# Hybrid decoder step on one core: expert outputs are added to the outputs by accumulating indirect DMAs instead of stored, gathered and combined

## The chip, the cores and the metric

The kernel runs on one core of a Trainium2 chip, in one launch. The time is that of the device in microseconds; of three runs of the kernel before the median is 1448.83 us (1443.56 to 1450.93). The core's engines work on instruction streams of their own and meet by semaphores: TensorE (PE in the rows) multiplies matrices, VectorE (DVE) and ScalarE (ACT) work on vectors, GpSimd (POOL) here mostly issues indirect DMAs, SyncE (SP) issues the direct ones. All DMAs move on the core's 16 DMA engines.

## The reference, cut to what matters

One layer of a decoder in float32 on 1024 prompt tokens and 64 sample tokens, width 1024: window attention and a convolution module, cross attention, then a mixture of experts. The change is in the last part:

```python
def hier_moe(h, w_rg, b_rg, w_re, b_re, w_gate, w_up, w_down):
    t = h.reshape(-1, D_MODEL)                       # 1088 tokens
    ...
    gate = jax.nn.softmax(top_v, axis=-1) * pg_sel   # top 1 of 4 groups, then top 2 of its 8 experts
    comb = jnp.einsum('tk,tke->te', gate, jax.nn.one_hot(eidx, N_EXPERTS))
    a = jnp.einsum('td,edf->tef', t, w_gate)         # 32 experts, 1024 -> 256
    b = jnp.einsum('td,edf->tef', t, w_up)
    act = jax.nn.silu(a) * b * comb[:, :, None]
    return jnp.einsum('tef,efd->td', act, w_down)    # 256 -> 1024
...
x = x + cross_attend(...)
x = x + hier_moe(rmsnorm(x, norm_ffn_g), ...)        # y_p (prompt), y_s (samples)
```

Each token has two experts, so 2176 rows of expert work come out, each scaled by its gate and added to its token's row of x.

## The kernel before, in words

Tokens come in 9 tiles (tile 0 the 64 samples, the others 128 prompt tokens each). Up to about 1017 us TensorE works through the projections, attention, convolution and cross attention. In the cross attention's loop each tile's logits go through the router on VectorE: `route_hot` finds the two experts, `route_rows` each row's rank within its expert (TensorE counts with triangular matrices), and `route_add` sums a table of which token stands at which rank of which expert. After the last tile the table is copied to `idx_i` and `route_ready` is signalled. The normalised rows lie in DRAM (`z3_scratch`), the residual x2 in SBUF and, for tiles 0 to 4, in `x2_scratch`.

The expert stage works in blocks of 128 rows. Four experts share three blocks: each of the first three has 96 rows of one block, the fourth ("shared") has the last 32 rows of all three. That makes 24 blocks. Rows beyond these 96 are overflow: 4 further blocks are always computed after the 24, and loops of up to 18 passes follow on each engine for overflow blocks that this input does not need.

For block n: GpSimd gathers 128 rows of z3 by `idx_i` (`gather`), TensorE transposes them (`turn_rows`, semaphore `zt4_done`), VectorE scales them (`take_rows`), TensorE multiplies gate and up weights (`gate_up`, 1 MB each per expert), ScalarE and VectorE make the activation (`activate`), TensorE transposes it and multiplies the down weights (1 MB, `down`), and ScalarE and VectorE copy half the output each into `YB[n%2]`. TensorE's program is interleaved: gate/up of block n+1, transposes of the activation of n, transposes of the rows of n+2, down of n. SyncE loads weights into four slots as they come free. It also stores `YB` into `y_scratch0..2` (8 blocks per scratch; the last one takes the rest), and fills the overflow part of the last scratch with zeros early in the kernel (11264 KB, line 494).

The combine pass: for each scratch, GpSimd gathers for each tile and each of the token's two experts the rows by `rows_i` into one of 6 buffers (`gather_y`), and VectorE adds gate times row to the tile in SBUF (`combine`, 54 in all). A token whose expert row lies in another scratch has an index out of bounds, and its row does not move. The passes over the first two scratches lie beside the blocks; the third follows the last block and SyncE stores each tile to the output. Gates, ranks and indices of the passes are computed by VectorE beside blocks 0 to 5 (`route_gates`, `route_slots`, `route_over`, `route_eids`, `route_passes`).

Of the kernel before, what the change touches and what calls it, by code (L numbers as in the profile page):

```python
# [6 lines left out]
D = 1024  # L7
# [18 lines left out]
EVEN, ODD = (NB + 1) // 2, NB // 2  # L26
PASSES, PER_PASS = 3, 8
CRING = 6
PAD_TOK, PAD_ROW = 4096.0, 60000.0
# [55 lines left out]

def weight_plan():
    need = []
    for q in range(NE // 4):
        need += [("e", 4 * q + 3)] + [("e", 4 * q + r) for r in range(3)]
    need += [("o", k) for k in range(STATIC_OVER)]  # L90
    uses = {}
    for n in range(NR):
        uses[n] = [("e", 4 * (n // 3) + n % 3), ("e", 4 * (n // 3) + 3)]
    for k in range(STATIC_OVER):
        uses[NR + k] = [("o", k)]
# [23 lines left out]
def build(nc, i, o):  # L119
# [7 lines left out]
    with ctx:  # L127
# [21 lines left out]
        gates = sb("gates", 2 * NT)  # L149
        idxs = sb("idxs", 4, i32)  # L150
        rows_i = sb("rows_i", PASSES * 2 * NT, i32)
# [91 lines left out]
        RO, RP3, RM, RR, RQ, IDXA = tt(2, NE), tt(2, NE), tt(NE), tt(2, 128), tt(2, NE), tt(NE)  # L243
# [9 lines left out]
        R_T9, R_PG, R_E2, R_EG = rt(NT), rt(NT), rt(NT), rt(NT, NG)  # L253
        R_CNT, R_GT, ROV, RBASE = rt(1), rt(8), rt(128), rt(33)
        R_RANK, R_EXP, R_BASE, R_FL, R_ROW = (rt(2 * NT) for _ in range(5))
        RE2, RG8, RE3, R_EID = rt(2 * NT, NE), rt(2 * NT, 8), rt(OVER, NE), rt(OVER)
        R_Q, R_LAST, R_PT = (rt(2 * NT) for _ in range(3))
        R_GE, R_PM = rt(PASSES + 1, 2 * NT), rt(PASSES, 2 * NT)
        assert _r[0] <= 4096
        RRO, RQO = view(G, 9216, 2 * NT, 128), view(G, 11520, 2 * NT, OVER)  # L260

        gm = dwT[:, 0:PASSES * 2 * NT]
# [10 lines left out]
        XS = [view(G, a, D) for a in (0, 1024, 2048, 3072, 8192)] + [XR[s % 4] for s in range(5, NT)]  # L273
        CY = [view(W, a + 1024 * r, D) for a in (12288, 28672, 36864) for r in range(2)]

# [4 lines left out]
        x2_d = nc.dram_tensor("x2_scratch", [NTOK, D], f32).ap()  # L280
        z3_d = nc.dram_tensor("z3_scratch", [NTOK, D], f32).ap()
        y_d = [nc.dram_tensor(f"y_scratch{g}", [PER_PASS * 128 + (OVER * 128 if g == PASSES - 1 else 0), D], f32).ap() for g in range(PASSES)]
# [4 lines left out]
        def tok_rows(t, s):  # L287

            return t[SEQ:NTOK, :] if s == 0 else t[(s - 1) * 128:s * 128, :]

# [7 lines left out]
        def ring(name, n):  # L298
# [15 lines left out]
            cy_used xs_in y_done dve""".split()}  # L314
# [67 lines left out]
        wgu_in, zg_in, y_out = ring("wgu_in", 4), ring("zg_in", 2), ring("y_out", 2)  # L382
        wdn_in, WDN_AFTER = wmk_in, 16
        cy_in = ring("cy_in", CRING)

        def comb_at(n):

            g, j = n // PER_PASS - 1, 3 * (n % PER_PASS - 2)
            return [] if g < 0 or g >= PASSES - 1 or j < 0 else [2 * NT * g + j + c for c in range(3)]
# [55 lines left out]
        def _(sp):  # L445
# [111 lines left out]
            for it in range(NT + 2):  # L557
# [23 lines left out]
                if 0 <= s2 < NT:  # L581
                    sp.wait_ge(M["x2_ready"], AFTER["x2_ready"] + 2 * s2 + 2)
                    if s2 <= 4:
                        sp.dma_start(tok_rows(x2_d, s2), XR[s2 % 4][0:rows_of(s2), :]).then_inc(x2_out[s2 % 4], 16)
# [15 lines left out]
            def store_y(n):  # L600
                sp.wait_ge(M["yb_readyA"], n + 1)
                sp.wait_ge(M["yb_readyD"], n + 1)
                g = min(n // PER_PASS, PASSES - 1)
                sp.dma_start(y_d[g][(n - PER_PASS * g) * 128:(n - PER_PASS * g + 1) * 128, :], YB[n % 2]).then_inc(y_out[n % 2], 16)

            over_e = {}

            def expert_id(w):
# [1553 lines left out]
```

## Time and profile before

| | |
|---|---|
| median of 3 runs | 1448.83 us |
| the profiled execution | 1450.07 us, span of its records 1448.2 us |
| TensorE busy | 1271.6 us, 88% |
| VectorE, ScalarE, GpSimd busy | 53%, 21%, 8% |
| moved by DMA | 238.27 MB |
| by the queue of GpSimd's DMAs | 17.85 MB |
| expert stage | 1038 to 1407 us |

The busy time of a matmul row is partly modelled. The span begins with the first instruction; all times in rows count from there. DMA share is the mean busy share of the 16 DMA engines.

### The profile page before, as it was taken

The page shows a single profiled execution, that of the slowest core. Times are in us where ns is not written, and L with a number is a line of the kernel's source. Part 1 is how long each engine was busy: PE and PEld are TensorE (multiplying, and loading weights), DVE is VectorE, ACT ScalarE, POOL GpSimd, SP SyncE. Part 2 cuts the span into 40 slices and gives each one's busy share as a digit, 9 for nine tenths or more (in the row PEclk, how much of TensorE's full clock was granted, in tenths as well). Part 3 has the DMA queues.
Part 4 walks back from the last instruction along what each step waited for, and adds up shares of the span by engine and source line. Part 5 has one row for each costly group of instructions (what it writes and reads, how often), then busy time and mean ns, then how long its engine had stood idle before and what let it go on. Part 6 is the DMA issues. An engine that isn't in the chain of part 4 may idle for free.

```text
span 1448.2 us, 17786 instructions
## 1 busy us (share of the span) xinstructions
PE 1271.6 (88%) x6455; PEld 644.4 (44%) x6455; DVE 768.9 (53%) x2207; ACT 308.5 (21%) x866; POOL 122.2 (8%) x171
## 2 busy tenths in 40 slices
PE   7989999999999767788999999997599999898970
PEld 3434545555455433443555655565333333233430
DVE  1118799999999981322444444453344224334416
ACT  1133344544453421120111111111001010011100
POOL 0000000000000001000000000000100032132104
PEclk9998999999999977898999999998699999999995
DMA  8796001200000302352005110001499999999916
GB/s 322 261 330 211 0 23 42 104 30 30 16 15 15 142 17 105 130 217 102 21 30 218 44 44 15 15 32 70 141 352 369 363 414 418 414 411 418 391 67 224
DMA packets 68320, 238.27 MB, mean 165 GB/s; under 512 B 14112, under 2 KB 28358, under 8 KB 54387
## 3 DMA queue, kind: packets, MB, share of 16 engines
q1 hardware_dynamic: 56235, 217.20, 39.2%
q0 software_dynamic: 11424, 17.85, 3.6%
q10 hardware_dynamic: 576, 2.10, 0.4%
q8 instruction: 52, 0.85, 0.2%
q14 instruction: 33, 0.27, 0.1%
HBM read 216.27 MB, written 45.77 MB: 181 GB/s over the span
## 4 chain that ended last, share of the span: by engine, by line
PE 69%; DVE 11%; DMA 7%; SPq 5%; issue 4%; ACT 3%; POOL 0%; DVEq 0%; POOLq 0%; ACTq 0%
PE bank L775 21%; PE bank L1194 12%; PE bank L1147 9%; PE bank L1201 7%; PE bank L976 4%; DVE W L1645 4%; SPq L496 3%; DMA W<-in_w_exp_down 3%; PE bank L1125 2%; PE bank L1085 2%; PE bank L1181 2%; PE bank L818 1%; DMA W<-in_w_mv 1%; DVE G L1589 1%; PE bank L1161 1%
## 5 line engine op out<-in xcount | busy, mean ns | idle before, releaser
L775 PE MATMUL bank<-W,G 128*128 128x512 f32 (+3 forms) x864 | 355.1, 567 | 4.2 <-DVE G L1589 3.4
L1645 DVE SCALAR_TENSOR_TENSOR W<-W,dwT 128x128 f32<-128x128 f32 (+1 forms) x1080 | 280.1, 336 | 0.0
L775 PEld LDWEIGHTS bank<-W,G 128*128 128x128 f32 (+1 forms) x864 | 158.9, 187 | 176.9 <-issue 170.7
L1194 PE MATMUL bank<-W 128*32 128x512 f32 (+1 forms) x1600 | 206.0, 611 | 12.7 <-issue 10.9
L976 PE MATMUL bank<-W 128*128 128x512 f32 (+1 forms) x288 | 130.2, 611 | 11.4 <-ACT W L1439 6.7
L1194 PEld LDWEIGHTS bank<-W 128*32 128x32 f32 (+1 forms) x1600 | 64.5, 116 | 149.5 <-issue 147.1
L1147 PE MATMUL bank<-W 128*128 128x512 f32 (+1 forms) x288 | 128.2, 599 | 0.8 <-DVE W L1907 0.6
L1201 PE MATMUL bank<-W 128*32 128x512 f32 (+1 forms) x800 | 107.2, 617 | 4.5 <-DMA W<-in_w_exp_down 3.6
L2078 DVE TENSOR_TENSOR W<-bank,cvec 128x512 f32<-128x512 f32 x56 | 36.3, 687 | 124.4 <-PE bank L1181 117.9
L976 PEld LDWEIGHTS bank<-W 128*128 128x128 f32 (+1 forms) x288 | 54.0, 190 | 81.6 <-issue 81.3
L664 POOL TENSOR_SCALAR st<-st 128x1 f32<-128x1 f32 (+3 forms) x41 | 8.0, 196 | 954.6 <-DVE st L1718 475.9
L1147 PEld LDWEIGHTS bank<-W 128*128 128x128 f32 (+1 forms) x288 | 52.0, 185 | 64.5 <-issue 64.4
L2092 DVE SCALAR_TENSOR_TENSOR G<-W,dwT,G 128x1024 f32<-128x1024 f32 (+1 forms) x54 | 69.0, 1277 | 18.0 <-issue 13.5
L2112 DVE COPY W<-bank 128x512 f32<-128x512 f32 x28 | 19.4, 692 | 111.3 <-PE bank L1201 103.4
L1537 ACT ACTIVATE W<-bank 128x256 f32<-128x256 f32 x28 | 10.8, 384 | 241.4 <-PE bank L1223 241.4
L715 POOL DMA_INDIRECT W<-y_scratch,rows_i x54 | 54.7, 1013 | 79.2 <-DMA y_scratch<-W 59.3
L1201 PEld LDWEIGHTS bank<-W 128*32 128x32 f32 (+1 forms) x800 | 29.7, 116 | 61.7 <-issue 60.2
L706 POOL DMA_INDIRECT W<-z_scratch,idx_i x28 | 27.9, 998 | 265.4 <-PE bank L1181 245.7
L1373 ACT ACTIVATE W<-W,st 128x256 f32<-128x256 f32 (+2 forms) x68 | 32.5, 478 | 49.4 <-DVE st L1699 49.4
L1474 ACT ACTIVATE W<-G 128x1024 f32<-128x1024 f32 (+1 forms) x9 | 9.5, 1057 | 151.1 <-DVE G L1966 151.1
L1911 DVE TENSOR_REDUCE st<-bank 128x2 f32<-128x512 f32 x16 | 11.1, 692 | 53.4 <-PE bank L1085 53.4
L1125 PE MATMUL bank<-W,G 128*128 128x128 f32 x256 | 33.2, 292 | 4.2 <-DVE W L1922 4.2
(294 smaller groups left out, 1374.4 us busy)
## 6 DMA issues: line engine op xcount, KB each, us to landing
W<-in_w_exp_gate SPq DMA_DIRECT2D x36, 1024.0 KB
W<-in_w_exp_up SPq DMA_DIRECT2D x36, 1024.0 KB
W<-in_w_exp_down SPq DMA_DIRECT2D x36, 1024.0 KB
y_scratch<-W SPq DMA_DIRECT2D x28, 512.0 KB
y_scratch<-LG SPq DMA_DIRECT2D x1, 11264.0 KB
W<-in_cache_mem_k SPq DMA_DIRECT2D x8, 1024.0 KB, 5.5
W<-in_cache_mem_v SPq DMA_DIRECT2D x8, 1024.0 KB, 8.1
W<-in_w_in SPq DMA_DIRECT2D x4, 1792.0 KB, 25.9
```

The source lines that it names most:

```text
L496: sp.dma_start(o["swa_k_s"][0, :, 0:128 - DEC_T], i["cache_swa_k"][0, :, DEC_T:128]).then_inc(M["moved_out"], 16)
L715: pool.indirect_dma_start(out=CY[q % CRING][0:rows_of(s), :], out_offset=None, in_=y_d[g], in_offset=bass.IndirectOffsetOnAxis(ap=rows_i[0 ...
L775: mm = pe.matmul(bank[0:rows, at:at + hi - lo], HT[:, c, 0:rows], w[:, c, lo:hi], start=(c == 0), stop=(c == DC - 1))
L976: mm = pe.matmul(B[half][0:n3, :], lhs, w_out[:, c, 512 * half:512 * half + 512], start=(c == 0), stop=(c == 7))
L1125: mm = pe.matmul(B[6 + c // 4][:, (c % 4) * 128:(c % 4) * 128 + 128], MV[:, mt, c * 128:(c + 1) * 128], PT2[:, mt, c // 2, :], start=(mt = ...
L1147: mm = pe.matmul(B[2 + half][0:n2, :], OT2[:, c, 0:n2], w_mo[:, c, 512 * half:512 * half + 512], start=(c == 0), stop=(c == DC - 1))
L1194: mm = pe.matmul(B[2 + par][lo:hi, :], HG[par][:, c, lo:hi], WGU[u][:, :, c, :], start=(c == 0), stop=(c == DC - 1), skip_group_check=True)
L1201: mm = pe.matmul(B[6 + half][lo:hi, :], AT[par][:, c, lo:hi], WD[u][:, c, 512 * half:512 * half + 512], start=(c == 0), stop=(c == 1), ski ...
L1373: act.activation(sh, sh, ACT.Exp, bias=st[:, 50 + h:51 + h], scale=SCALE, accum_out=st[:, 58 + h:59 + h]).then_inc(M["s_exp"], 2 if s2 == ...
L1645: dve.scalar_tensor_tensor(y, src, w, y, ALU.mult, ALU.add).then_inc(M["conv_tap"], 1)
L2078: dve.tensor_tensor(buf[:, 4 * half:4 * half + 4, :], B[half][:, :].rearrange("p (c t) -> p c t", c=4), gain(V_FFN + 4 * half, 4), ALU.mul ...
L2092: dve.scalar_tensor_tensor(XS[s][0:n, :], CY[q % CRING][0:n, :], gm[0:n, at:at + 1], XS[s][0:n, :], ALU.mult, ALU.add).then_inc(M["cy_used ...
```

## The change

1. The rows of x2 of all nine tiles are stored directly to the outputs `y_p` and `y_s` (`y_rows`). Expert rows are then added there: `add_rows` issues two indirect DMAs with `compute_op=ALU.add` from `YB`, one into the 1024 rows of the prompt's output, one into the 64 rows of the samples'. Each skips the rows whose index is out of its bounds. `y_scratch`, `rows_i`, `gather_y`, `combine`, the reload of x2, the final stores and the zero fill are gone.
2. A token's two rows must not be added at once, so an expert block is added in two parts (rows 0 to 95 by `idx_i`/`samp_i`; then all 128 with an index table `part_i` that is out of bounds in the first 96), and each part waits until all adds before have landed (`yp_added`, `ys_added`). Overflow blocks go in one part. GpSimd adds block n-3 in its step n, behind the gather for block n+2.
3. ScalarE and VectorE wait for the adds of block n-2 before they write `YB[n%2]`, where they waited for its store.
4. The gate is multiplied into the activation (`activate`, `gate_s`). For this it is computed for each tile in the router (`gate_exp` on ScalarE, five steps in `route_rows`) and carried in the table beside the token; the steps after the last tile grow by the samples' index, the parts' indices and the gates.
5. The four overflow blocks stand after the fourth to the seventh group of three (`block_order`), with the weight loads in that order; SyncE frees the down weights' slot on `dn_done` instead of the output copies.

```diff
+def block_order():
+    order = []
+    for q in range(NE // 4):
+        order += [("e", 3 * q + r) for r in range(3)]
+        if 3 <= q < 3 + STATIC_OVER:
+            order.append(("o", q - 3))
+    return order
...
+        def parts_of(n):
+
+            return [(0, 128)] if BLOCKS[n][0] == "o" else [(0, WIDE), (WIDE, 128)]
+
+        def adds_through(n):
+
+            return sum(len(parts_of(m)) for m in range(n + 1))
...
-            sp.wait_ge(M["dve"], 1)
-            zeros = LG[:, None, 0:256].to_broadcast([128, OVER * 4, 256])
-            sp.dma_start(y_d[PASSES - 1][PER_PASS * 128:, :].rearrange("(p n) (q d) -> p (n q) d", p=128, d=256), zeros).then_inc(M["moved_out"], 16)
...
+            def add_rows(lo, hi, at_p, at_s, buf):
+
+                pool.indirect_dma_start(out=yp_flat, out_offset=bass.IndirectOffsetOnAxis(ap=at_p, axis=0), in_=buf[lo:hi, :], in_offset=None,
+                                        bounds_check=SEQ - 1, oob_is_err=False, compute_op=ALU.add).then_inc(M["yp_added"], 16)
+                pool.indirect_dma_start(out=ys_flat, out_offset=bass.IndirectOffsetOnAxis(ap=at_s, axis=0), in_=buf[lo:hi, :], in_offset=None,
+                                        bounds_check=NS - 1, oob_is_err=False, compute_op=ALU.add).then_inc(M["ys_added"], 16)
+
+            def add_block(n):
+
+                at, done = block_column(n), adds_through(n - 1) if n else 0
+                pool.wait_ge(M["yb_readyA"], n + 1)
+                pool.wait_ge(M["yb_readyD"], n + 1)
+                for lo, hi in parts_of(n):
+                    if done:
+                        pool.wait_ge(M["yp_added"], 16 * done)
+                        pool.wait_ge(M["ys_added"], 16 * done)
+                    if lo:
+                        add_rows(0, hi, part_i[:, at:at + 1], part_i[:, NR + at:NR + at + 1], YB[n % 2])
+                    else:
+                        add_rows(0, hi, idx_i[0:hi, at:at + 1], samp_i[0:hi, at:at + 1], YB[n % 2])
+                    done += 1
...
-            for n in range(NB - 2):
-                pool.wait_ge(M["zt4_done"], 2 * n + 2)
-                gather(idx_i[:, n + 2:n + 3], zg_in[n % 2], ZG[n % 2])
-                for q in comb_at(n):
...
+            for n in range(NB + 3):
+                if n + 2 < NB:
+                    pool.wait_ge(M["zt4_done"], 2 * n + 2)
+                    if BLOCKS[n + 2] == ("o", 0):
                         pool.wait_ge(M["over_ready"], 1)
+                    at = block_column(n + 2)
+                    gather(idx_i[:, at:at + 1], zg_in[n % 2], ZG[n % 2])
+                if n == 3:
+                    pool.wait_ge(M["gate_ready"], 1)
+                    for k in range(4):
+                        pool.wait_ge(x2_out[k], 16 * len(range(k, NT, 4)))
+                if n >= 3:
+                    add_block(n - 3)
...
+            def gate_exp(s4):
+
+                lg = LG[0:rows_of(s4), 36 * s4:36 * s4 + 36]
+                act.wait_ge(M["r_hot"], AFTER["r_hot"] + s4 + 1)
+                act.activation(T_EXP[0:rows_of(s4), :], lg[:, 0:NG], ACT.Exp, accum_out=T_GATE[0:rows_of(s4), 0:1])
+                act.activation(T_GATE[0:rows_of(s4), 1:2], lg[:, 4:5], ACT.Exp).then_inc(M["r_exp"], 1)
...
                 if n >= 2:
-                    act.wait_ge(y_out[p], (n // 2) * 16)
+                    act.wait_ge(M["yp_added"], 16 * adds_through(n - 2))
+                    act.wait_ge(M["ys_added"], 16 * adds_through(n - 2))
...
+            def activate(p, e, a, gate):
+
+                return dve.scalar_tensor_tensor(by_row(a, 2), B[2 + p][:, FE:2 * FE].rearrange("p (f c) -> p f c", c=2), gate,
+                                                e.rearrange("p (f c) -> p f c", c=2), ALU.mult, ALU.mult)
```

GpSimd's program in the middle of the expert stage, before: `zt4_done` is the transposes of an earlier block's rows, `cy_used` a combine on VectorE that frees a buffer.

```order
L706 DMA W<-z_scratch,idx_i 128x1024 [waits zt4_done] x11
L715 DMA W<-y_scratch,rows_i 64x1024 [waits y_out1,y_out0,over_ready]
L715 DMA W<-y_scratch,rows_i 64x1024
L715 DMA W<-y_scratch,rows_i 128x1024
L706 DMA W<-z_scratch,idx_i 128x1024 [waits zt4_done]
L715 DMA W<-y_scratch,rows_i 128x1024 x3
L706 DMA W<-z_scratch,idx_i 128x1024 [waits zt4_done]
L715 DMA W<-y_scratch,rows_i 128x1024 [waits cy_used] x3
```

And now, from the fourth block's gather on: `yp_added` and `ys_added` are the landings of the adds before.

```order
L701 DMA W<-z_scratch,idx_i 128x1024 [waits zt4_done] x4
L707 DMA out_y_p<-W,idx_i 1024x1024 [waits x2_out3,x2_out2,yb_readyA,x2_out1,yb_readyD,x2_out0,gate_ready]
L709 DMA out_y_s<-W,samp_i 64x1024
L707 DMA out_y_p<-W,part_i 1024x1024 [waits ys_added,yp_added]
L709 DMA out_y_s<-W,part_i 64x1024
L701 DMA W<-z_scratch,idx_i 128x1024 [waits zt4_done]
L707 DMA out_y_p<-W,idx_i 1024x1024 [waits yp_added,ys_added,yb_readyD,yb_readyA]
```

In place of one gather and, in some steps, three gathers of outputs, each step of GpSimd holds a gather and four adding DMAs, the third behind a wait for the first two and the next step's first behind a wait for the last two.

GpSimd's end of the program, before: the body's end and the closing of the loop over further overflow blocks (L739, L740; `idxs` is the index column of such a block), and what follows it.

```order
L706 DMA W<-z_scratch,idxs 128x1024 [waits idx_copied]
L746 ISA
L740 UNCONDITIONAL_BRANCH [waits y_out0]
L739 REGISTER_ALU
L739 COMPARE_AND_BRANCH
L715 DMA W<-y_scratch,rows_i 64x1024 [waits cy_used,y_out1,y_out0]
L715 DMA W<-y_scratch,rows_i 64x1024 [waits cy_used]
L715 DMA W<-y_scratch,rows_i 128x1024 [waits cy_used] x16
L127 UNCONDITIONAL_BRANCH
```

And now, the last block's adds, the reading of the number of blocks (L748) and the entry of the loop (L749, L750), behind whose close only the final branch is left.

```order
L707 DMA out_y_p<-W,part_i 1024x1024 [waits ys_added,yp_added]
L709 DMA out_y_s<-W,part_i 64x1024
L748 TENSOR_LOAD eid_i [waits zg_in0,zt4_done,ys_added,yp_added]
L748 ISA x2
L749 UNCONDITIONAL_BRANCH
L750 COMPARE_AND_BRANCH
L751 ISA
```

The 18 gathers behind the loop are gone; the loop itself, which stood ahead of the last stores' landing, now stands behind the landing of the last adds.

## Rows read from the trace of the kernel before

**Rows 1.** The page's busy line and its chain that ended last, by engine.

```profile
PE 1271.6 (88%) x6455; PEld 644.4 (44%) x6455; DVE 768.9 (53%) x2207; ACT 308.5 (21%) x866; POOL 122.2 (8%) x171
...
PE 69%; DVE 11%; DMA 7%; SPq 5%; issue 4%; ACT 3%; POOL 0%; DVEq 0%; POOLq 0%; ACTq 0%
```

**Rows 2.** Stretches: from:to, length, busy time by engine, PE clock, DMA share, GB/s.

```profile
1038.00:1407.00 369.00, 346.34 (x2708) 128.93 (x2708) 133.60 (x237) 35.29 (x84) 61.13 (x62) 0.96 0.89 355
1052.00:1352.00 300.00, 281.97 (x2454) 101.82 (x2446) 117.41 (x213) 28.90 (x69) 58.17 (x59) 0.97 0.99 395
1040.00:1060.00 20.00, 19.06 (x166) 6.42 (x162) 3.12 (x5) 1.20 (x3) 1.98 (x2) 0.94 0.53 190
1352.00:1400.00 48.00, 46.08 (x158) 21.14 (x154) 13.56 (x19) 5.07 (x13) 0.99 (x1) 1.00 0.53 217
1406.00:1448.20 42.20, 0.00 (x0) 0.00 (x0) 23.68 (x19) 0.00 (x0) 19.29 (x18) 0.56 0.62 207
```

**Rows 3.** Timeline of TensorE, one block: start, duration, line, [idle before <- releaser].

```profile
1061.04 7.05 PE L1194 MATMUL bank<-W 128*32 128x512 f32 x64
...
1068.29 1.04 PE L1181 MATMUL bank<-cst,W 128*128 128x128 f32 x8
...
1072.71 7.05 PE L1194 MATMUL bank<-W 128*32 128x512 f32 x64
```

**Rows 4.** Timeline of the tail: last output copy, first gather, first combine.

```profile
1405.90 0.69 DVE L2112 COPY W<-bank 128x512 f32<-128x512 f32 x1 [6.47 <-PE bank L1201]
1410.13 0.93 POOL L715 DMA_INDIRECT W<-y_scratch,rows_i  x1 [48.07 <-DMA y_scratch<-W]
...
1420.12 16.56 DVE L2092 SCALAR_TENSOR_TENSOR G<-W,dwT,G 64x1024 f32<-64x1024 f32 x12 [13.53 <-issue]
```

**Rows 5.** The zero fill: SyncE's next issue, ScalarE's wait, and two stretches.

```profile
77.62 41.53 SPq L496 DMA_DIRECT2D out_swa_k_s<-in_cache_swa_k  x1
...
132.93 1.06 ACT L1285 ACTIVATE W<-G 128x1024 f32<-128x1024 f32 x1 [16.39 <-DMA G<-in_x_prompt]
...
100.00:120.00 20.00, 15.57 (x112) 8.94 (x111) 12.95 (x53) 8.26 (x25) 0.00 (x0) 0.74 1.08 376
120.00:140.00 20.00, 19.10 (x56) 10.00 (x54) 19.13 (x95) 5.98 (x11) 0.00 (x0) 1.00 0.54 171
```

**Rows 6.** Timeline of GpSimd: one of several indirect DMAs in a row.

```profile
1340.26 0.99 POOL L715 DMA_INDIRECT W<-y_scratch,rows_i  x1 [0.30 <-issue]
```

**Rows 7.** Direct DMAs: KB each and median landing; the block stores by their line.

```profile
G<-x_scratch SPq DMA_DIRECT2D x12, 512.0 KB, 4.3
...
z_scratch<-W SPq DMA_DIRECT2D x8, 512.0 KB, 2.9
...
L604 SPq DMA_DIRECT2D y_scratch<-W x28: 326/327/349, 1062.1 to 1406.7; - x28
```

**Rows 8.** Landing of z gathers (L706): from 1000 to 1040, 1040 to 1060, all.

```profile
DMA to landing us min/median/max: 4.9/4.9/4.9
...
DMA to landing us min/median/max: 7.9/7.9/7.9
...
DMA to landing us min/median/max: 4.9/9.0/11.4
```

**Rows 9.** Timelines of VectorE, ScalarE and TensorE around the router's steps.

```profile
830.24 0.69 DVE L1927 COPY W<-bank 128x512 f32<-128x512 f32 x1 [2.12 <-PE bank L1125]
...
1024.95 0.19 DVE L1815 TENSOR_TENSOR W<-W 128x32 f32<-128x32 f32 x1
...
1026.37 0.22 DVE L1824 TENSOR_TENSOR W<-W,bank 128x64 f32<-128x64 f32 x1 [1.15 <-PE bank L1019]
...
1029.76 0.17 DVE L1850 CAST idx_i<-W 96x24 int32<-96x24 f32 x1
...
1029.29 0.23 ACT L1528 ACTIVATE G<-LG 128x36 f32<-128x36 f32 x1 [18.42 <-DVEq L2072]
...
1035.44 1.94 PE L1181 MATMUL bank<-cst,W 128*128 128x128 f32 x8 [4.08 <-DMA W<-z_scratch,idx_i]
```

More of the change, by code:

```diff
@@ L83, in rows_of, with block_column @@
     return NS if s == 0 else 128
-def weight_plan():
[L87 to L95, printed above, removed]
+def block_order():
[5 more added lines that the diff above has]
+    return order
+BLOCKS = block_order()
+def block_column(n):
+    kind, k = BLOCKS[n]
+    return k if kind == "e" else NR + k
+def weight_plan():
+    need, uses = [], {}
+    for n, (kind, k) in enumerate(BLOCKS):
+        if kind == "o":
+            uses[n] = [("o", k)]
+        else:
+            uses[n] = [("e", 4 * (k // 3) + k % 3), ("e", 4 * (k // 3) + 3)]
+        need += [w for w in reversed(uses[n]) if w not in need]
     last = {w: n for n, ws in uses.items() for w in ws}
@@ L620, in _ @@
             for n in range(NB):
-                if n == OVER_AT + 2:
-                    sp.wait_ge(M["over_ready"], 1)
-                    for s in range(5):
-                        sp.dma_start(XS[s][0:rows_of(s), :], tok_rows(x2_d, s)).then_inc(M["xs_in"], 16)
                 if n + 1 < NB and FREED[n + 1]:
@@ L1466, in _ @@
                     sum_sq(NT + 2, rows_of(0), XR[0])
[L1469 to L1471 removed]
+            def gate_exp(s4):
[3 more added lines that the diff above has]
+                act.activation(T_GATE[0:rows_of(s4), 1:2], lg[:, 4:5], ACT.Exp).then_inc(M["r_exp"], 1)
+            for it in range(NT + 3):
+                s1, s2, s3, s4 = it, it - 1, it - 2, it - 3
+                if 0 <= s4:
+                    gate_exp(s4)
+                if 0 <= s3 < NT:
                     n3 = rows_of(s3)
@@ L1814, in route_hot @@
                     link(dve.tensor_tensor(RO[0:n, k, :].rearrange("p (g e) -> p g e", g=NG), bc(og, EPG, 2), bc(T_O[0:n, k, :], NG, 1), ALU.mult))
+                link(dve.tensor_tensor(lg[:, 4:5], top[:, 2:3], top[:, 1:2], ALU.subtract))
                 dve.tensor_tensor(RM[0:n, :], RO[0:n, 0, :], RO[0:n, 1, :], ALU.add).then_inc(M["r_hot"], 1)
-                dve.tensor_tensor(lg[:, 4:5], top[:, 2:3], top[:, 1:2], ALU.subtract).then_inc(M["dve"], 1)
-                steps[0] += 1
             def route_rows(s4):
                 n = rows_of(s4)
-                keep = LG[0:n, 36 * s4 + 5:36 * s4 + 9]
+                keep, gate = LG[0:n, 36 * s4 + 5:36 * s4 + 9], LG[0:n, 36 * s4 + 9:36 * s4 + 11]
+                part = T_GATE[0:n, :]
+                dve.wait_ge(M["r_exp"], AFTER["r_exp"] + s4 + 1)
+                link(dve.tensor_scalar(part[:, 2:3], part[:, 1:2], 1.0, part[:, 0:1], ALU.add, ALU.mult))
+                link(dve.reciprocal(gate[:, 0:1], part[:, 2:3]))
+                link(dve.tensor_tensor(gate[:, 1:2], gate[:, 0:1], part[:, 1:2], ALU.mult))
+                for k in range(2):
+                    link(dve.tensor_scalar(RQ[0:n, k, 1, :], RO[0:n, k, :], gate[:, k:k + 1], None, ALU.mult))
+                link(dve.tensor_scalar(RQ[0:n, :, 0, :], RO[0:n], tok[0:n, s4:s4 + 1], None, ALU.mult))
                 dve.wait_ge(M["r_rank"], AFTER["r_rank"] + s4 + 1)
```

237 lines of the change are left out of this document (84 added, 153 removed).

## The prediction, as it was recorded before the changed kernel ran

> **What bounds the kernel now.** I read the page's busy shares and chain first, then the stretches, the timeline of one block, the landings of the indirect gathers, and last the two places where the removed passes show. TensorE is busy 88% and holds 69% of the chain [rows 1]. The expert stage runs from 1038 to 1407 us: TensorE is busy 346.3 of 369 us, so it idles 22.7 there, with the DMA engines at a share of 0.89, and of 0.99 from 1052 to 1352 [rows 2]. A block of expert rows costs TensorE 11.7 us (gate/up starts at 1061.04, the next at 1072.71) [rows 3]. After the last block comes a tail without TensorE, 42.2 us [rows 2]: the last copy at 1405.90 (0.69 us), 13.53 us in which VectorE only runs through its loop over overflow blocks that don't occur, then the last combine pass [rows 4].
>
> **What is removed.** (a) The tail's combine: from 1420.1 to 1448.2, 28 us. (b) 54 gathers and 54 combines, 28 stores of 512 KB (14.7 MB), and the zero fill of 11.5 MB. In the stage the combines lie beside TensorE; what they cost is within the 22.7 us of idle time. (c) The zero fill blocks SyncE for 41.53 us, and ScalarE waits 16.39 us for a prompt tile behind it, but TensorE is busy 15.57 and 19.10 us of the 20 in the two stretches around it [rows 5]; its idle there is mostly after VectorE rows. I count 1 us gained (bounds 0 and 5.3, all the idle time of the two stretches).
>
> **What is added.** Each block's output is now added from SBUF into the two output tensors by GpSimd. The 24 expert blocks come in two parts (rows 0 to 95, then the shared expert's 32), the 4 overflow blocks in one: 52 parts, each of two DMAs, one into the prompt's output and one into the samples', most of whose rows are out of bounds. Before each part GpSimd waits until both adds of the part before have landed. Queued behind that wait are the other part, the gather for a later block, and with it everything: ScalarE and VectorE may only write block n's output when the adds of block n-2 have landed, VectorE's next activation stands behind that copy, and TensorE's transposes behind the activation.
>
> So a chain of its own arises on GpSimd. Let t be the time from the issue of a part's first add to the landing of its second. A block takes 2t plus one gather's issue, 0.99 + 0.30 = 1.3 us [rows 6]; TensorE takes 11.7. The chain decides if t is over 5.2 us. **What t is** no row of before shows, so it is bounded:
> - from below: two issues are 1.3 us apart [rows 6], and a plain store releases its waiter 3.4 us after its issue on idle DMA engines (1406.7 to 1410.13) [rows 4, 7]. 4.7 us.
> - from above: 1.3 us plus the slowest gather, 11.4 us [rows 8]. 12.7 us. A read-modify-write that takes a gather and then a store one after the other would be 1.3 + 9.0 + 3.4 = 13.7.
> - near rows: the same kind of indirect DMA, a gather of 128 rows, lands 4.9 us after issue when the engines are nearly idle, 7.9 us in the stretch from 1040 to 1060, where the DMA share is 0.53, 9.0 in the median [rows 2, 8]. So already the pair of weight loads that belongs to a block makes it slow.
>
> With t = 8 an expert block takes 17.3 us. Three of them use four experts, 12.6 MB, so 243 GB/s of weights, and adds and gathers on top: which makes about 290: a share of some 0.7 where 395 GB/s go with 0.99 [rows 2], between the rows of 7.9 and 9.0 us. Against that: a part moves at most 96 or 32 rows where a gather has 128, and a plain store lands in 2.9 us where a plain load of that size takes 4.3 [rows 7]. For more: the second add's 1.3 us, the gather queued ahead, the tiny packets of out-of-bounds rows, and the reading of the destination. I take t = 8, by the 7.9 row.
>
> The Trainium skill ("DMA: Bandwidth & Descriptors", section "Anatomy of one DMA") gives a GpSimd DMA about 2.0 us plus bytes over 436 GB/s; for 96 rows of 4 KB that would be an estimated 2.9 us, t near 4 and no GpSimd chain at all, which is the first rival. The trace disagrees as far as it goes: the gather's 4.9 and 9.0 us [rows 8] stand against its 3.2 for 128 rows. The same page, section "Queues, rings and completion order", lets each DMA engine go round its queues packet by packet; by that, light packets still wait their turns behind weight packets, and t stays near 8 although few bytes move.
>
> **The router's additions.** Gates are now computed for each tile: 2 exponentials on ScalarE (one of 0.23 us stands in the rows) and 5 small VectorE steps of about 0.2 us. For eight tiles they fit in VectorE's 2.12 us of idle time before its copy at 830.24. For the last they stand on the path: the mask leaves at 1025.1, VectorE goes on at 1026.37; exponentials and five steps would end about 1 us later. Then come 16 small copies of 0.17 us, 2.8 us, and route_bases, some ten steps; TensorE waits for the first gather until 1035.44 anyway [rows 9]. Cost 1 us (bounds 0 and 3.8). Of route_slots and route_passes many steps go; what TensorE waited for them goes too, but under a GpSimd chain it is worth nothing, for what is late next is the adds. The same holds for the overflow blocks placed between the groups: it evens the weight loads (their share is 0.53 after 1352 against 0.99 before [rows 2]), a gain only if TensorE or weights decide.
>
> **The sum**, on the profiled execution: the transposes of block 3 end at 1069.3 [rows 3]; router +1, a gather's issue +1.3: the first add goes out at 1071.6. Then 52 t, and 23 gathers x 1.3 = 29.9. Behind the last landing GpSimd still runs its loop over absent overflow blocks; I take VectorE's 13.5 us for it [rows 4], bounds 5 and 20. Zero fill -1, outside the span +1.9 (1450.07 less 1448.2; that execution is 1.2 over the median of the runs). Together 1115.9 + 52 t: for t = 8, 1532 us. It meets 1450 at t = 6.43, so the cost of the change is almost wholly 52 times what t exceeds 6.4.
>
> **Rivals.**
> 1. Adds are cheap, t of 5.2 or less, TensorE stays the bound. For: the 4.9 us gather, the 2.9 us stores, 14.7 MB less stored. Against: all landings of 7.9 and more beside weights. Time: last copy at 1406.6, less most of the 22.7 us idle (17), router +1: 1390.6; then two parts of 5 and the loop, 1414; with -1 and +1.9, 1415 us. Between t = 5.2 and 6.3 the chain decides and the time, up to 1443 us, is still below before. Faster.
> 2. A read-modify-write costs both trips, t = 13.7: 1828 us; from t = 11 on (1688) I count this case. For: the destination is read first, and nothing in the trace shows an accumulating DMA. Against: reading and writing of many rows overlap in each gather too.
> 3. The blocks' lag of three and the chain balance, t 6.3 to 6.55: no change, within 0.5% of the time (7 us, about what a measurement of this kernel can tell). That the adds fail to replace the passes is no rival: the diff leaves no combine.
>
> **Chances.** My forecast, t from 6.55 to 11, 1457 to 1688: 0.64, likeliest about 1530; its own range is 1475 to 1640. Rival 2, 0.11. Rival 3, 0.04. Faster by over 0.5% (rival 1 with its band), 0.21: that this band is not smaller comes from the two rows for idle engines, since a slower stage also loads them less. Slower by over 0.5% is 0.64 + 0.11 = 0.75. The range 1412 to 1680 leaves out about 1 in 10 above and the lower half of rival 1 below.
>
> **What would show it.** Right: GpSimd's adds follow at about 8 us a pair, ScalarE's and VectorE's waits before the output copies fall on the adds' DMAs, TensorE's rows come every 17 us with waits before the transposes of the activation, the DMA share in the stage is about 0.7, weights are never waited for, and after the last add there is a stretch of some 13 us without work. Wrong: TensorE at 11.7 us a block with adds landing within 5 us (rival 1), or a DMA share below 0.5 and pairs 13 us apart (rival 2). If t is as forecast but the total is not, the GpSimd loop or the 1 us terms are off.

## The result, and the profile after

The changed kernel takes 1564.54 us in the median of 4 runs (1559.12 to 1569.9), the kernel before 1447.98 (4 runs beside them): a ratio of 1.0813, 95% interval 1.079 to 1.0835. The forecast was 1532 with a range of 1412 to 1680, and slower by over 0.5% at 0.75. The profiled execution took 1569.9 us, its span is 1567.8. The executions of one kernel given here lie within 1% of one another, so where a time below comes from one run, a difference of 56 us or more is far outside that.

The page's busy line, then its chain of work by engine and by line:

```profile
PE 1293.0 (82%) x6455; PEld 654.9 (42%) x6455; DVE 717.2 (46%) x2206; ACT 311.5 (20%) x891; POOL 226.3 (14%) x221
...
DMA 0%
DMA out_y_s<-W,part_i 0%
```

GpSimd (POOL) works 226 us where it worked 122, and VectorE 52 us less [rows 1]: the combines are gone. The page's chain, which before gave TensorE 69%, now names one single add and stops there, so it says nothing of the stage. (It does so in the runs without the empty loop too; why is not known.) A chain that breaks off like this is a reason to go to the waits. These are the waits from 1030 us on (engine, tile and line that waited; releaser; us in total, times, longest):

```profile
ACT W L1560 <- DMA out_y_s<-W,part_i: 309.6, 21, 22.2
DVE W L2103 <- DMA out_y_s<-W,part_i: 277.3, 21, 20.9
...
POOL out_y_p L707 <- DMA out_y_s<-W,samp_i: 133.7, 22, 11.3
POOL out_y_p L707 <- DVE W L2103: 120.3, 23, 9.4
PE bank L1236 <- DVE W L2086: 111.1, 21, 12.9
```

Read from below upwards this is the chain that was forecast: TensorE's transposes of the activation wait for VectorE's activation, that stands behind VectorE's output copy (L2103), and this waits for the adds of two blocks back, as ScalarE's copy (L1560) does. GpSimd waits between the parts of a block for an add. Between blocks the profile names VectorE's copy, but that is the copy of a later block, for which GpSimd doesn't wait: the landing that released the copy is the one that GpSimd waited for (below). No wait for weights is in the whole list.

The chain itself on GpSimd, in the first two blocks and at the end (start, duration, line, [idle before it <- releaser]):

```profile
1071.55 0.99 POOL L701 DMA_INDIRECT W<-z_scratch,idx_i  x1 [10.69 <-PE bank L1194]
1072.84 1.49 POOL L707 DMA_INDIRECT out_y_p<-W,idx_i  x1 [0.30 <-issue]
1074.63 1.43 POOL L709 DMA_INDIRECT out_y_s<-W,samp_i  x1 [0.30 <-issue]
1087.35 1.56 POOL L707 DMA_INDIRECT out_y_p<-W,part_i  x1 [11.29 <-DMA out_y_s<-W,samp_i]
1089.21 1.56 POOL L709 DMA_INDIRECT out_y_s<-W,part_i  x1 [0.30 <-issue]
1091.08 1.06 POOL L701 DMA_INDIRECT W<-z_scratch,idx_i  x1 [0.30 <-issue]
1098.89 1.46 POOL L707 DMA_INDIRECT out_y_p<-W,idx_i  x1 [6.75 <-DVE W L2103]
...
1534.81 1.56 POOL L707 DMA_INDIRECT out_y_p<-W,part_i  x1 [4.59 <-DMA out_y_s<-W,samp_i]
1536.68 1.56 POOL L709 DMA_INDIRECT out_y_s<-W,part_i  x1 [0.30 <-issue]
1540.78 1.42 POOL L707 DMA_INDIRECT out_y_p<-W,idx_i  x1 [2.54 <-DMA out_y_s<-W,part_i]
1542.51 1.42 POOL L709 DMA_INDIRECT out_y_s<-W,samp_i  x1 [0.30 <-issue]
1547.35 1.56 POOL L707 DMA_INDIRECT out_y_p<-W,part_i  x1 [3.42 <-DMA out_y_s<-W,samp_i]
1549.22 1.56 POOL L709 DMA_INDIRECT out_y_s<-W,part_i  x1 [0.30 <-issue]
```

The landings of the adds into the samples' output (L709), those of the adds into the prompt's (L707), and ScalarE's copy that waited for the same landing as GpSimd's issue at 1098.89:

```profile
DMA to landing us min/median/max: 2.7/6.1/11.9
...
DMA to landing us min/median/max: 2.7/6.2/11.7
...
1098.08 0.60 ACT L1560 ACTIVATE W<-bank 128x512 f32<-128x512 f32 x1 [16.07 <-DMA out_y_s<-W,part_i]
```

Four things stand in these rows. An adding DMA occupies GpSimd for 1.42 to 1.56 us, the gather for 0.99 to 1.06. From the first add of a part to the first add of the next it takes 14.5, 11.5 us beside weights, 6.0 and 6.6 us at the end, where the weights are all in. A landing is not yet the next issue: the add of 1089.21 lands 8.8 us later, at 1098.0, ScalarE starts at 1098.08, and GpSimd's next add at 1098.89, 0.9 us after the landing; over all parts this step takes 0.84 us at least and 0.89 in the mean. And nothing follows 1549.22 until the span's end at 1567.8. Counted to where a next issue would begin, the last part ends at about 1553.3, if it takes the 4.1 us of the row 1536.68 to 1540.78; so 52 parts take 1553.3 - 1072.84 = 480.5 us, 9.24 us each, and 14.5 us without work follow.

The stage until 1500 (from:to, length, busy time of TensorE, weight loads, VectorE, ScalarE, GpSimd, then TensorE's granted clock, DMA share, GB/s):

```profile
1038.00:1500.00 462.00, 353.09 (x2607) 136.94 (x2609) 89.62 (x186) 32.14 (x77) 161.45 (x115) 0.87 0.73 252
```

TensorE now idles 109 of 462 us and its granted clock is 0.87 instead of 0.96 [rows 2]. The lower clock goes with the gaps: from 1085 to 1093 us it is 1.00, while TensorE waits until 1104.7 it is 0.50, and in the 7.3 us of work behind that 0.70. TensorE's rows behind a gap take longer for it (below), but TensorE waits after them all the same, so the clock is not what sets the time.

TensorE, one block (start, duration, line, [idle before it <- releaser]):

```profile
1085.84 7.05 PE L1207 MATMUL bank<-W 128*32 128x512 f32 x64
1104.79 0.69 PE L1236 MATMUL bank<-cst,W 128*128 128x128 f32 x2 [11.90 <-DVE W L2086]
1105.28 1.91 PE L1194 MATMUL bank<-cst,W 128*128 128x128 f32 x8
1107.12 4.57 PE L1214 MATMUL bank<-W 128*32 128x512 f32 x32
```

Against [rows 3], gate/up (64 matmuls) still take 7.05 us, but behind them TensorE waits 11.9 us; after that wait the eight transposes take 1.91 us instead of 1.04 and the down product 4.57 where 3.64 is common. The wait is a long one because in this block VectorE also runs some 5.3 us of routing steps between its copy (1098.09) and the activation; in the mean of the waits listed above it is 5.3 us. From the first block's add (1072.84) to the last's (1540.78) it is 467.9 us for 27 blocks: 17.3 us a block.

### The profile page after: what moved, and what is told of

The parts are those of the page before. It is cut to its first block and busy times, and to the rows that moved or that the text cites. A ratio compares the mean times of both kernels' runs of the same rounds, so it can differ in the third digit from the quotient of the medians.

```text
span 1567.8 us, 17872 instructions
## 1 busy us (share of the span) xinstructions
PE 1293.0 (82%) x6455; PEld 654.9 (42%) x6455; DVE 717.2 (46%) x2206; ACT 311.5 (20%) x891; POOL 226.3 (14%) x221
## 3 DMA queue, kind: packets, MB, share of 16 engines
q0 software_dynamic: 17472, 17.92, 5.6%
## 5 line engine op out<-in xcount | busy, mean ns | idle before, releaser
L1207 PE MATMUL bank<-W 128*32 128x512 f32 (+1 forms) x1600 | 200.2, 599 | 1.7 <-DVE W L2082 1.7
L2103 DVE COPY W<-bank 128x512 f32<-128x512 f32 x28 | 19.3, 691 | 318.5 <-DMA out_y_s<-W,part_i 277.3
L1214 PE MATMUL bank<-W 128*32 128x512 f32 (+1 forms) x800 | 116.7, 665 | 0.9 <-ACT W L1554 0.9
L1236 PE MATMUL bank<-cst,W 128*128 128x128 f32 x56 | 15.4, 367 | 111.1 <-DVE W L2086 111.1
L1560 ACT ACTIVATE W<-bank 128x512 f32<-128x512 f32 x28 | 16.7, 597 | 352.8 <-DMA out_y_s<-W,part_i 309.6
L1236 PEld LDWEIGHTS bank<-cst,W 128*128 128x128 f32 x56 | 7.0, 170 | 135.3 <-DVE W L2086 131.7
L707 POOL DMA_INDIRECT out_y_p<-W,idx_i x28 | 41.7, 1489 | 129.0 <-DVE W L2103 120.3
L707 POOL DMA_INDIRECT out_y_p<-W,part_i x24 | 37.6, 1565 | 145.5 <-DMA out_y_s<-W,samp_i 133.7
L1194 PE MATMUL bank<-cst,W 128*128 128x128 f32 x224 | 41.1, 345 | 1.0 <-DMA W<-z_scratch,idx_i 1.0
L709 POOL DMA_INDIRECT out_y_s<-W,samp_i x28 | 40.4, 1444 | 8.5 <-issue 8.5
## 6 DMA issues: line engine op xcount, KB each, us to landing
W<-in_w_mv SPq DMA_DIRECT2D x4, 1024.0 KB, 13.5
```

What stands on the lines that cost most here:

```text
L707: pool.indirect_dma_start(out=yp_flat, out_offset=bass.IndirectOffsetOnAxis(ap=at_p, axis=0), in_=buf[lo:hi, :], in_offset=None, bounds_ch ...
L709: pool.indirect_dma_start(out=ys_flat, out_offset=bass.IndirectOffsetOnAxis(ap=at_s, axis=0), in_=buf[lo:hi, :], in_offset=None, bounds_ch ...
L1194: mm = pe.transpose(B[half][:, c * 128:(c + 1) * 128], ZG[u][:, k * 128:(k + 1) * 128], ident)
L1207: mm = pe.matmul(B[2 + par][lo:hi, :], HG[par][:, c, lo:hi], WGU[u][:, :, c, :], start=(c == 0), stop=(c == DC - 1), skip_group_check=True)
L1214: mm = pe.matmul(B[6 + half][lo:hi, :], AT[par][:, c, lo:hi], WD[u][:, c, 512 * half:512 * half + 512], start=(c == 0), stop=(c == 1), ski ...
L1236: mm = pe.transpose(B[4 + p][:, c * 128:(c + 1) * 128], AB[p][:, c * 128:(c + 1) * 128], ident)
```

## The experiments

**One part for each block.** The 52 parts exist because a block's rows 0 to 95 and its last 32 (the shared expert) can hold the same token, and the change keeps a token's two rows out of one DMA. Here the last 32 rows come from the group of experts two further on, whose tokens are others, so one part will do: 28 parts, the same rows and bytes. The filling of the second parts' index columns goes too.

```diff
-            uses[n] = [("e", 4 * (k // 3) + k % 3), ("e", 4 * (k // 3) + 3)]
+            uses[n] = [("e", 4 * (k // 3) + k % 3), ("e", 4 * ((k // 3 + 2) % 8) + 3)]
...
-            return [(0, 128)] if BLOCKS[n][0] == "o" else [(0, WIDE), (WIDE, 128)]
+            return [(0, 128)]
...
-                    a = dve.tensor_copy(slots[WIDE:128, :, r], table[PART * r:PART * r + PART, :, 3])
+                    dve.tensor_copy(slots[WIDE:128, 0:6, r], table[PART * r:PART * r + PART, 2:8, 3])
+                    a = dve.tensor_copy(slots[WIDE:128, 6:8, r], table[PART * r:PART * r + PART, 0:2, 3])
```

> The changed kernel, but the shared expert of each group of three blocks is taken from the other expert group two places on, so that no token stands twice in a block and every block is added in one part: 28 parts in a chain instead of 52, the same rows. If the chain of parts on GpSimd decides (9.2 us a part now), a block needs one part and a gather's issue, 9 to 11 us, which is less than TensorE's 11.7: TensorE decides again, last output copy near 1395, then a part and the loop, 1405 to 1445 us. Rival: the adds cost by rows and bytes (read-modify-write), not by their number; 2176 rows stay, and the time stays at 1540 to 1570.

Measured: 1434.7 us (1431.41 to 1435.84, 4 runs), ratio to the kernel before 0.990, interval 0.9861 to 0.9939, a gain of 1%; 130 us less than the changed kernel, in the expected range. Its adds into the prompt's output, and its stretch of the stage:

```profile
L707 POOL DMA_INDIRECT out_y_p<-W,idx_i x28: 1552/1579/2158, 1074.1 to 1413.6; - x28
...
DMA to landing us min/median/max: 4.7/10.0/12.2
...
1038.00:1400.00 362.00, 341.93 (x2681) 125.70 (x2679) 90.59 (x189) 34.27 (x82) 107.93 (x77) 0.96 0.88 324
```

A block now takes (1413.6 - 1074.1) / 27 = 12.6 us, against TensorE's 11.7 [rows 3] and the 9 to 11 expected: the chain is still slightly longer than TensorE's work, and ScalarE's and VectorE's copies still wait for adds. The add even lands later (10.0 us in the median; 6.2 in the changed kernel). It has 128 rows where it had 96 or 32, and the DMA share is 0.88 where it was 0.73; which of the two makes it later was not tried apart. But there is one landing a block and not two. The count of landings in a row decides, for the rows that move and their bytes are the same. (The rows out of bounds, of which the second parts had many, fall too; the run with four targets below keeps them all and gains as much.)

**Only the prompt's adds.** Of the pair of DMAs of each part the one into the samples' output is left out, so that output lacks its experts' rows; the waits for it go with it.

```diff
-                pool.indirect_dma_start(out=ys_flat, ... compute_op=ALU.add).then_inc(M["ys_added"], 16)
```

> The changed kernel without the adds into the samples' output (the expert rows of the 64 sample tokens are left out); still 52 parts in a chain, each of one DMA. If a part costs two issues of 1.45 to 1.56 us and the landing of the second, each part falls by one issue and its gap, 1.8 us, and perhaps some of the landing: 52 x 1.8 to 2.5 us, so 1435 to 1470 us. Rival: the landing of the first, larger add decides and the second hides behind it; then less than 20 us go.

Measured: 1508.87 us in one run, 56 less than the changed kernel, 1.07 us a part. A miss for the expectation (1435 to 1470) and for its rival (less than 20 us): the step from one DMA to two was put too high. The adds that are left land in 7.3 us in the median where those into the prompt's output took 6.2 with the second behind them. The stage runs faster, its DMA share from 1038 to 1400 us rises from 0.75 to 0.81, and part of the saving is given back. In this run the page's chain doesn't break off: it gives TensorE 53% and DMAs 26%, where it gave 69% and 7% before [rows 1].

**Plain writes in place of adds.** The same DMAs without accumulation; where two blocks write a row, the last one stands and the sums are missing.

```diff
-                                        bounds_check=SEQ - 1, oob_is_err=False, compute_op=ALU.add).then_inc(M["yp_added"], 16)
+                                        bounds_check=SEQ - 1, oob_is_err=False).then_inc(M["yp_added"], 16)
```

> The changed kernel with the same indirect DMAs as plain writes (rows overwrite the outputs instead of being added), the same waits. If accumulating costs only the longer issue (1.45 to 1.56 against 1.0 us for a gather), parts fall by some 1 us and the time to 1505 to 1530. Rival: reading the destination first makes the landing; then each landing falls by 2 us or more and the time to below 1470. Second rival: nothing changes (1555 to 1570), the wait is that of any scatter.

Measured: 1505.48 us in one run, 59 less, the lower edge of the expected range. Its rows by line, and its end:

```profile
L707 POOL DMA_INDIRECT out_y_p<-W,idx_i x28: 917/928/1472, 1074.2 to 1481.4; - x28
L707 POOL DMA_INDIRECT out_y_p<-W,part_i x24: 982/988/1000, 1088.4 to 1486.1; - x24
...
DMA to landing us min/median/max: 2.1/6.0/11.4
...
1481.41 0.92 POOL L707 DMA_INDIRECT out_y_p<-W,idx_i  x1 [2.02 <-DMA out_y_s<-W,part_i]
...
1486.07 0.98 POOL L707 DMA_INDIRECT out_y_p<-W,part_i  x1 [2.52 <-DMA out_y_s<-W,samp_i]
1487.36 0.98 POOL L709 DMA_INDIRECT out_y_s<-W,part_i  x1 [0.30 <-issue]
```

Issues take 0.92 to 0.98 us, some 0.5 less than the adding ones. Beside weights the landing, counted from the issue's start, has nearly the same median (6.0 against 6.2); its mean is 5.9 against 6.9, and half of this 1.0 us is the longer issue itself. On idle DMA engines a part takes 4.7 us here (1481.41 to 1486.07) and 6.6 with adds (1540.78 to 1547.35): 1.0 of these 1.9 us are the two issues, 0.9 is left for the accumulation. With a last landing 3.0 us after 1487.36 (as from 1478.41 to 1481.41, one part earlier), the 52 parts take (1490.4 - 1074.2) / 52 = 8.0 us each, against 9.24. So accumulation, its longer issues included, is some 60 us of the time, and the chain of landings the larger rest: plain writes in the same chain are still 4% slower than the kernel before.

**Four targets.** The parts add in turn into four scratch tables, and a part waits for the part four back, so that no two DMAs in flight write the same table; the tables are not brought together at the end, so the expert rows are missing from the outputs.

```diff
-                    if done:
-                        pool.wait_ge(M["yp_added"], 16 * done)
-                        pool.wait_ge(M["ys_added"], 16 * done)
+                    if done >= 4:
+                        wait_part(pool, done - 4)
```

> The changed kernel with its 52 parts of two adds, but part j goes into scratch j mod 4 (the outputs keep x2 alone, the four sums are not brought together), so that GpSimd waits for the part four back instead of the last one; number, size, kind and queue of the DMAs stay. If the wait for the last landing makes the time, GpSimd needs 4 x 1.8 + 1.4 = 8.6 us a block, TensorE's 11.7 decide again, and the time is 1410 to 1440 us. Rival: the DMA engines can't do these adds faster beside the weights; then the time stays above 1520.

Measured: 1439.3 us in one run. GpSimd in the middle of the stage:

```profile
1197.80 1.46 POOL L718 DMA_INDIRECT tp_scratch<-W,idx_i  x1 [0.31 <-issue]
1199.56 1.43 POOL L720 DMA_INDIRECT ts_scratch<-W,samp_i  x1 [0.30 <-issue]
1201.29 1.57 POOL L718 DMA_INDIRECT tp_scratch<-W,part_i  x1 [0.30 <-issue]
1203.16 1.56 POOL L720 DMA_INDIRECT ts_scratch<-W,part_i  x1 [0.30 <-issue]
1210.27 1.06 POOL L712 DMA_INDIRECT W<-z_scratch,idx_i  x1 [5.54 <-PE bank L1204]
```

All 104 accumulating DMAs are still there, with the same issue times, and those into the prompt's tables land in 12.8 us in the median of the 39 whose landing the trace tells; but four go out back to back, and GpSimd then waits for TensorE (PE) and not for a landing. The page's chain gives TensorE 67% again. That is worth 125 us. It is the wait for each landing before the next issue that costs the time. (The four tables also change where rows are added; this can't be told apart from the shorter waits here.)

**No weights in the stage.** The weight loads of blocks after the first ones are left out (the matmuls run on stale weights).

```diff
-                for w in FREED[n]:
-                    load_down(sp, expert_id(w), WSLOT[w])
```

> The changed kernel without the weight loads of the expert stage: each block works on what lies in its slot (wrong experts for most), all else as before. If the landing is long because light packets share the DMA engines with the weights, a part falls from 9.2 us to the 6.5 us seen where nothing else moves, 52 x 2.7 = 140 us less: 1420 to 1455 us. Rival: a landing of 6 us belongs to the add itself; then the time stays above 1530.

Measured: 1437.8 us in one run, 127 less than the changed kernel. GpSimd, the landings of the prompt's adds, and the stretch:

```profile
1207.06 1.46 POOL L701 DMA_INDIRECT out_y_p<-W,idx_i  x1 [1.21 <-DVE W L2097]
...
1213.38 1.56 POOL L701 DMA_INDIRECT out_y_p<-W,part_i  x1 [3.13 <-DMA out_y_s<-W,samp_i]
...
1220.17 1.46 POOL L701 DMA_INDIRECT out_y_p<-W,idx_i  x1 [2.00 <-DVE W L2097]
...
DMA to landing us min/median/max: 2.7/5.0/6.6
...
1038.00:1400.00 362.00, 339.52 (x2710) 124.53 (x2708) 91.89 (x191) 35.30 (x84) 175.60 (x124) 0.96 0.27 47
```

These parts take 6.3 and 6.8 us from issue to next issue (1207.06, 1213.38, 1220.17); all take 6.7 in the mean and 8.5 at most, and the slowest landing is 6.6 us, against 11.7. A block takes 12.4 us, near TensorE's 11.7, and the time is 0.6% below that of the kernel before beside it (1446.49). The rest, 9.24 - 6.7 or 2.5 us a part, is the neighbourhood of the weights. It also speaks against the first rival: from a part's first issue to its second landing it takes 5.7 us in the mean, so that the rival's 5.2 isn't reached even on nearly idle engines, at a DMA share of 0.27.

**Overflow blocks last.** The four overflow blocks come behind the 24 others and not between the groups.

```diff
-        if 3 <= q < 3 + STATIC_OVER:
-            order.append(("o", q - 3))
+    order += [("o", k) for k in range(STATIC_OVER)]
```

> The changed kernel with the four overflow blocks after the 24 others again (only their order is undone). The number of parts is the same, so if the chain decides, the time stays within 8 us of 1564. Rival: spread weights shorten the landings, or the overflow blocks' order costs; then it moves by more than 10 us.

Measured: 1565.12 us (1558.79 to 1569.38, 4 runs), ratio to before 1.0808, interval 1.0774 to 1.0841; the changed kernel's is 1.0813. No difference, as expected: weight loads are not what is waited for, so their order is worth nothing here.

**The empty loop skipped.** On every engine the loop over further overflow blocks stands in a condition.

```diff
+            with pool.If(total > 1):
-            with pool.Fori(1, OVER - STATIC_OVER + 1) as n:
+                with pool.Fori(1, OVER - STATIC_OVER + 1) as n:
```

> The changed kernel with the loops over further overflow blocks inside one condition on each engine, so that they are passed over when there is none. If the 14 us after the last add are GpSimd's loop of 18 empty passes, the time falls by 12 to 14 us, to 1550. Rival: they are the landing of the last adds and the end of the program, and at most 2 us go.

Measured: 1554.25 us (1549.94 to 1557.56, 4 runs), ratio to before 1.0723 (1.068 to 1.0767), 10.3 us less than the changed kernel. In the trace the last add's issue is at 1547.07 and the span ends at 1555.5: 8.4 us later, in place of 18.6. Landing (4.1) and some 4 us of ending are left. So the loop is worth 10 us and not the 12 to 14 expected, and of the 14.5 us behind the last part 4 belong to what follows the loop.

**Both together.** One part for each block, and the loop skipped.

> One part per block (as in the run before of that name, 1434.7 us) and the loops over further overflow blocks behind one condition. The two act at different places (the chain of adds; the stretch behind the last add), so the condition gives again what it gave alone, 10 us: 1422 to 1428 us, faster than the kernel before by 1.5 to 2%. Rival: with the chain shorter another engine's loop or the end of the program holds the end, and less than 4 us come.

Measured: 1427.97 us (1425.74 to 1432.26, 6 runs), ratio to before 0.9876, interval 0.9854 to 0.9897: 1.2% less than the kernel before, at the upper edge of the expected range. The guard adds 3.5 to 7 us to the run with one part (by the ratios, by the medians), less than the 10 us that it gave alone. Its last issue on GpSimd, and the stage until 1400:

```profile
1415.89 1.55 POOL L710 DMA_INDIRECT out_y_s<-W,samp_i  x1 [0.30 <-issue]
...
1038.00:1400.00 362.00, 337.90 (x2642) 126.23 (x2642) 89.67 (x187) 33.02 (x79) 106.94 (x77) 0.96 0.89 324
```

TensorE is busy 338 of 362 us. The stage is no shorter than before: VectorE's last output copy begins at 1410.56, where it began at 1405.90 [rows 4]. What is saved is the tail: the last add goes out at 1415.89 and the span ends at 1426.0, where before the last combine pass and its stores held until 1448.2 [rows 2, 4].

**The same guard on the kernel before.** The loops skipped in the kernel before, nothing else, to see whose gain that is.

> The kernel before, with its loops over further overflow blocks skipped when there are none (the guard of e7 and e9), nothing else. It tells how much of e9's gain over the kernel before belongs to the adding DMAs and how much to the skipped loop. Theory A, from before's tail: VectorE's first combine starts at 1420.12 after 13.53 us in the loop, GpSimd's seventh gather of the last pass waits for the buffer that this combine frees (4.68 us), and the first six gathers need until 1417.5; without the loop the combine can start at about 1414, when the first gathers have landed, so GpSimd goes on without a gap and the end comes 4 to 6 us earlier: 1442 us (1440 to 1445). e9 then stays some 14 us faster than this. Rival: the loop is on the path with its whole 13.5 us, 1435 us, and more than half of e9's gain would be the guard. Second rival: nothing, since the gathers and the last stores set the end, 1448.

Measured: 1449.23 us (1446.1 to 1453.59, 12 runs), ratio 0.9993, interval 0.998 to 1.0007: nothing, the second rival of this expectation and not the 4 to 6 us of its main theory. Its tail:

```profile
1412.68 2.66 DVE L2096 SCALAR_TENSOR_TENSOR G<-W,dwT,G 64x1024 f32<-64x1024 f32 x2 [7.11 <-DMA W<-y_scratch,rows_i]
1412.97 1.87 POOL L716 DMA_INDIRECT W<-y_scratch,rows_i  x1 [0.30 <-issue]
...
1419.94 1.95 POOL L716 DMA_INDIRECT W<-y_scratch,rows_i  x1 [0.30 <-issue]
...
1436.13 1.08 POOL L716 DMA_INDIRECT W<-y_scratch,rows_i  x1 [0.30 <-issue]
```

VectorE's first combine starts at 1412.68 instead of 1420.12, as that theory had it (about 1414), and GpSimd no longer waits for a buffer. But its issues, which before took 0.93 to 1.14 us apart from the one behind the wait (1.46), now take up to 1.95 in the part where VectorE's combines run between them, and the last gather goes out at 1436.13, where it was 1437.85. The 13.53 us of [rows 4] were off the path: GpSimd's 18 gathers are the path there. So the guard gives the kernel before nothing, and the version with one part gains 1% without it (0.990); with the adds the loop stands on the path, and only there does the guard count. Why the issues stretched was not tried apart, nor was the other choice of shared experts on the kernel before.

## Why the prediction was right, and by how much it was off

**The mechanism** was as forecast, in each step: the adds form a chain on GpSimd of 52 parts; ScalarE's and VectorE's waits stand before the output copies; TensorE's rows come every 17.3 us (17 forecast) with waits before the transposes; the DMA share is 0.73 (0.7); weights are not waited for; the end is a stretch without work of 14.5 us (13.5). Three experiments cut the chain in different ways and each gives back 125 to 130 us: fewer landings, landings not waited for one by one, quicker landings.

**The sum** was 38 us short of the profiled 1569.9. By its terms: first add out at 1072.84, where router and zero fill together gave 1070.6 (+2.2); 52 parts with their gathers 480.5 us, where 52 x 8 + 29.9 = 445.9 were put (+34.6); the stretch behind them +1.0; outside the span +0.2.

- **t as it was defined** runs from a part's first issue to the landing of its second add. It was put at 8 and is 8.35 us in the mean of the 52 parts (4.6 to 13.7), +18 us together. This agreement is in part luck. The 8 was the landing of one gather, 7.9 us, and the second issue's offset stood only under "for more". Measured, that offset is 1.8 us (1072.84 to 1074.63) and not 1.3, because an accumulating issue is 0.5 us longer, and the second add lands 6.5 us after it in the mean.
- **From landing to the next issue** GpSimd needs 0.9 us, 46 us for 52 parts, and the sum had nothing for it. Of the forecast's numbers only the plain store's 3.4 us, used in its bounds, held this step, as they ran from the store's issue to its waiter's start; a gather's landing ends before it. So a link of the chain costs 8.35 + 0.89 = 9.24 us.
- **The 23 gathers at 1.3 us** were a double count. The gather's issue stands behind the second part's issue (1091.08 to 1092.14 in the rows above) and runs while that part lands; it lengthens a block only if the landing is shorter than it. This +29.9 hid nearly half of the error of the two points above (18 + 46): without it the forecast would have been 1502. That the sum is near with errors both ways is luck in its size, though not in its sign.
- **The break-even** was put at t = 6.43 with the gathers' 29.9 us, so at 7.0 us a part in all. With the measured other terms it is 6.9 from issue to next issue, near that. Without weights a part takes 6.7, just below, and the time is 1437.8, just below the kernel before.
- **The loop's 13.5 us** were right in their sum and not in what they are: skipping it gives 10 us, and some 4 us of ending, for which the forecast had no term, make up the rest.
- **Bounds of t.** 4.7 us, the lower end, was built without an accumulating issue; plain writes reach just this from issue to next issue (1481.41 to 1486.07), the adds of the changed kernel took 6.0 and 6.6 on idle engines. The upper rivals' 13.7 was reached by single parts (the first, 1072.84 to 1086.5) but not by the mean.
- **Router +1.** TensorE now waits 4.8 us for VectorE's routing step, then 1.0 for the gather, where it waited 1.6 and 4.1 us [rows 9]:

```profile
1035.05 0.63 PE L1185 MATMUL bank<-W,G 32*128 32x33 f32 x2 [4.84 <-DVE G L2014]
1036.64 1.94 PE L1194 MATMUL bank<-cst,W 128*128 128x128 f32 x8 [0.96 <-DMA W<-z_scratch,idx_i]
```

  The first transposes start at 1036.64, before at 1035.44: +1.2.
- **Zero fill -1.** TensorE's stretches there (100 to 120 and 120 to 140 us) after, against [rows 5]:

```profile
100.00:120.00 20.00, 15.57 (x115) 9.16 (x114) 13.14 (x54) 11.87 (x33) 0.00 (x0) 0.74 0.15 38
120.00:140.00 20.00, 19.48 (x73) 10.47 (x72) 19.44 (x95) 4.29 (x18) 0.00 (x0) 1.00 0.00 0
```

  The DMA engines are free (share 0.15 and 0.00, where it was 1.08 and 0.54), ScalarE's 16 us wait is gone, and TensorE gains 0.4 us here. At 150 us its blocks come 2.4 us earlier than before, but at 682 nothing is left of it: later waits take it back. Neither the 1 us nor its upper bound of 5.3 reached the end.

**Open.** Why landings beside weights lie between 2.7 and 11.7 us: the share of the DMA engines and the landing rise together (share 0.27 with 5.0 us, 0.73 with 6.2, 0.88 with 10.0 in the run with one part for each block), but packets' places in the queues are not seen in these views. Whether reading the destination or the adding makes up the 0.9 us of accumulation wasn't tried.

## What to carry to other kernels

Count the DMAs that wait for one another, and take each at its issues, plus the landing beside the traffic that will be there, plus the step from that landing to the next issue (0.9 us here); the bytes they save don't enter. An accumulating scatter can replace a combine pass with a small gain (1% here) if rows that could meet are kept out of one DMA by the layout (here other experts' rows in a block), so that a block needs one landing and not two. Before crediting a gain to a guard or a shorter loop, try it on the old kernel alone: it may have been off the path there.

## What the runs showed of the hardware

- An indirect DMA with accumulation occupies GpSimd for 1.42 to 1.58 us in the changed kernel (once 2.02), the same DMA without it for 0.92 to 1.00 (once 1.47); on idle DMA engines the second of a pair releases its waiter 4.8 us after its issue begins (1542.51 to 1547.35), without accumulation 3.4.
- From the landing of a DMA to the start of the indirect DMA that waits for it, GpSimd takes 0.84 us at least and 0.89 in the mean.
- A DMA of 96 or 128 rows most of which are out of bounds (into the samples' output) lands in 6.1 us in the median, hardly sooner than the one that carries the rows (6.2). A row out of bounds still makes a packet: the queue of GpSimd's DMAs counts 17472 packets in the changed kernel, which are the 15360 rows of its 132 indirect DMAs, in bounds or not, and 16 for each DMA; the counts of the kernel before (11424) and of the run with one part (12096) come out in the same way.
- The empty loop of 18 passes costs GpSimd some 10 us with nothing else to do.
- GpSimd's gather issues rose from about 1.1 to 1.95 us in a stretch where VectorE's combines alternated with them. In the kernel before they took 1.1 us beside combines too, so the cause is open.
